# Two transformer layers on eight cores: background weight casts issued by a running account instead of by step counters, with the small loads around them moved

## Chip, cores, metric

One Trainium2 chip, all 8 cores, one launch. Each core takes one sample of the batch and runs the same program on it; nothing is exchanged. The metric is device time in microseconds (us) of the slowest core. Every core reads its weights from the chip's memory (HBM) itself, so the eight load at the same moments.

## The reference, cut to what matters

```python
for l in range(DEPTH):                                   # 2 layers; D=1024, 2048 latent + 256 context tokens
    sh1, sc1, g1, sh2, sc2, g2 = adaln(c, ada_w[l], ada_b[l])       # silu(c) @ w + b, six vectors; same for c_ctx
    mix_lat, mix_ctx = hybrid_mixer(modulate(x, ...), modulate(ctx, ...), ...)
    #  one input projection, 4 heads differential attention (2 softmax maps each, keys = latent + context)
    #  beside 4 heads bidirectional mLSTM (conv, gates, chunked scan); one output projection
    x = x + g1 * mix_lat
    x = x + g2 * channel_mixer(modulate(x, norm2_g[l], sh2, sc2), l, ...)
    #  layer 0: swiglu, D_FF=2816;  layer 1: top-2 of 8 experts, D_FF_EXPERT=3584
    ...                                                  # context tokens likewise, in layer 0 alone
```

The arithmetic is in bfloat16 on TensorE; all weights arrive as float32.

## The kernel before

**Stages.** Eight blocks of the modulation matrix and the input tokens are loaded, then each layer runs: `attn` (projection, norm and rotation of q and k in jobs of one head and one token tile, v in 18 blocks, then the attention proper), `w_out_half` (the attention half of the output projection), `mlstm` (eight projections `p` with a convolution each, gates, v and output gate blocks, then the scan of 18 chunks in two directions, which is 36 units `u` and 4 to drain), `w_out_norm` (the other half, together with the next norm). Layer 0 ends with `ffn_dense`, layer 1 with `moe_sparse`, in which tokens are routed by a float32 product with the router weights `wr`, scattered to slots in HBM (`xslots`), and 23 tiles of 256 slots go through the experts.

**The attention proper** walks over steps `g`: one step is one block of 128 keys against a tile of 512 queries of one head. TensorE makes two score blocks, ScalarE the exponential over both, TensorE eight products with `vaug`. A full tile is 18 steps; in layer 0 a context tile of 2 steps follows every four. Layer 0 has 296 steps, layer 1 has 288. At a tile's end VectorE divides by the sums (its `RECIPROCAL`, one in each tile). In layer 0 one of the 16 remaining blocks of the modulation matrix (`ada_half`, 16 small matmuls and a VectorE add) is worked in after every 17th step, from a single buffer `adaw` in the `attr` area: the load of the next one is issued right behind it.

**Background casts.** The experts' weights are needed in bfloat16, but come in float32. `precast` lets a DMA on the GpSimd (POOL) queue copy one block of 128x4096 from HBM to HBM and convert it: 2 MB read and 1 MB written. There are 168 of them (21 blocks of 8 experts), and the first load of an expert tile waits for the last. Each cast waits on POOL for the TensorE instruction recorded just before it, so it is issued where it stands in TensorE's order. Where they stand is set by counters in each loop: every fourth attention job, every 12th step in layer 0 and every 7th in layer 1, one after most projections `p`, every third scan unit up to `u` 27, one before each strip of the dense FFN, and so on. Whatever is left when `moe_sparse` begins is issued there in one go.

**Queues.** Weight loads (`wslot`, `fslot`, `adaw`, with a conversion to bfloat16) are issued on POOL too, in program order between the casts, and so are the `iota` table and `wr` at the start of `moe_sparse`, behind the casts that are left. SP has the input tokens, `lam`, the zero-fill of `xslots` (11.8 MB written from a small constant), and then the experts' weights. SP's instructions wait only for their own buffers: the zero-fill stands in `attn` of layer 1, but reads a constant that was loaded at the start.

A `fence` makes the named engines wait for all compute recorded so far. TensorE takes `wslot` slots in turn: in `mlstm` the projections with `p` from 4 on need the load of `w_in` group 4, which is issued at the start of `mlstm`, behind the casts of the attention.

## Time and profile before

| | us |
|---|---|
| median of 3 runs (lowest, highest) | 4913.67 (4563.16, 5036.57) |
| profiled execution | 4566.67 |
| its span on core 7, the slowest | 4565.6 |
| spans of the other cores | 4525.7 to 4563.2 |
| TensorE busy on core 7 | 3878.8 (85%) |
| VectorE, ScalarE, GpSimd busy | 1505.7, 1522.5, 523.0 |
| chain that ended last | PE 73%, ACT 7%, issue 6%, DVE 6%, DMA 4% |

The profile is one execution, and all rows below are of core 7 unless they say otherwise. "Issue" as a releaser is idle time of an engine for which the profile shows no wait. "Us to landing" of a DMA runs from its issue to its last byte. The experts' part begins near 2800 us and is the last 1,700 us of the span; all that is changed lies ahead of it.

### The profile page before, as it was taken

What the parts mean: (1) busy time and instruction counts of PE and PEld (TensorE: products, weight loads), DVE (VectorE), ACT (ScalarE), POOL (GpSimd) and SP (SyncE); (2) the same over time, 40 slices, a digit from 0 to 9 for tenths busy, and PEclk for the clock granted to TensorE, in tenths of its full rate; (3) what the DMA queues carried; (4) which work ended last, traced back from release to release, by engine and by line L of the source; (5) the groups of instructions that cost most, each with busy time, mean ns of one, the idle gap of its engine ahead of it and who ended that gap; (6) DMA issues with size and microseconds to landing.
All of it is one profiled execution on the core that took longest, in us unless ns stands there. A gap on an engine that the chain in (4) does not pass through costs nothing.

```text
span 4565.6 us, 77498 instructions; the slowest of 8 cores (4525.7 to 4565.6 us)
## 1 busy us (share of the span) xinstructions
PE 3878.8 (85%) x28584; PEld 2519.2 (55%) x28584; DVE 1505.7 (33%) x2750; ACT 1522.5 (33%) x2399; POOL 523.0 (11%) x634
## 2 busy tenths in 40 slices
PE   4788889657999979888695376999999999999994
PEld 2345545433444434554344255777777778787773
DVE  3634452673223264334127232111111111111114
ACT  4678822554010277884126231111111111111110
POOL 0210000540000012000007212000000000000003
PEclk8999999868999999998896567999999999999997
DMA  9586653648884526999947507999999999999997
GB/s 240 86 111 107 107 93 65 93 65 120 120 113 81 97 44 91 110 109 109 118 65 98 74 1 264 312 310 318 308 320 306 320 307 321 304 320 310 312 309 248
DMA packets 112689, 822.84 MB, mean 180 GB/s; under 512 B 14496, under 2 KB 14768, under 8 KB 41408
## 3 DMA queue, kind: packets, MB, share of 16 engines
q0 software_dynamic: 31392, 280.83, 40.2%
q1 hardware_dynamic: 80928, 537.05, 35.0%
q8 instruction: 237, 3.88, 0.4%
q14 instruction: 132, 1.08, 0.1%
HBM read 1016.79 MB, written 217.06 MB: 270 GB/s over the span
## 4 chain that ended last, share of the span: by engine, by line
PE 73%; ACT 7%; issue 6%; DVE 6%; DMA 4%; POOL 2%; another core or an unknown queue 2%; DVEq 0%; ACTq 0%; POOLq 0%; SPq 0%
PE psall L273 65%; PE psall L270 5%; ACT attr L298 4%; PE psall L277 2%; DMA adaw<-ada_w 2%; DMA xstage<-x 1%; DVE ntmp L301 1%; DVE attr L334 1%; ACT hT L298 1%; DVE attr L301 1%; POOL wslot L301 1%; DMA attr<-ada_w 1%; POOL sigt L301 1%; ACT wslot L298 1%
## 5 line engine op out<-in xcount | busy, mean ns | idle before, releaser
L273 PE MATMUL psall<-hs,mslot 128*128 128x256 bf16 x10304 | 1130.6, 273 | 0.5 <-ACT hs L332 0.5
L273 PEld LDWEIGHTS psall<-hs,mslot 128*128 128x128 bf16 x10304 | 1009.2, 98 | 123.0 <-issue 0.7
L298 ACT ACTIVATE sig<-psall 128x512 bf16<-128x512 f32 x322 | 192.2, 597 | 1444.7 <-PE psall L273 1444.7
L298 ACT ACTIVATE attr<-psall 128x1024 bf16<-128x1024 f32 (+1 forms) x660 | 592.1, 979 | 183.0 <-PE psall L273 180.4
L273 PE MATMUL psall<-mslot,ysp 128*128 128x512 bf16 x2576 | 559.7, 379 | 0.0
L301 DVE TENSOR_TENSOR ysp<-sig,psall 128x512 bf16<-128x512 bf16 x322 | 221.3, 687 | 866.4 <-PE psall L273 844.0
L270 PE MATMUL psall<-vaug,attr 128*128 128x129 bf16 x4640 | 393.1, 228 | 61.8 <-issue 29.3
L273 PEld LDWEIGHTS psall<-mslot,ysp 128*128 128x128 bf16 x2576 | 251.2, 98 | 298.5
L270 PEld LDWEIGHTS psall<-vaug,attr 128*128 128x128 bf16 x4640 | 278.0, 100 | 209.0 <-issue 207.4
L273 PE MATMUL psall<-hT,fslot 128*128 128x512 bf16 (+1 forms) x1760 | 352.0, 363 | 0.9 <-ACT ftf L298 0.9
L273 PE MATMUL psall<-hT,wslot 128*128 128x512 bf16 (+1 forms) x1248 | 282.6, 373 | 41.4 <-DMA wslot<-w_in 36.0
L273 PE MATMUL psall<-catA,kT 64*128 64x512 bf16 (+1 forms) x1440 | 272.6, 374 | 26.5 <-ACT attr L298 12.6
L273 PEld LDWEIGHTS psall<-hT,fslot 128*128 128x128 bf16 x1760 | 172.9, 99 | 176.6 <-issue 11.1
L328 DVE SCALAR_TENSOR_TENSOR xT<-psall,mod,xT 128x512 f32<-128x512 f32 (+1 forms) x264 | 185.7, 709 | 247.4 <-PE psall L273 237.9
L301 DVE TENSOR_TENSOR otok<-psall,g2b 128x512 bf16<-128x512 f32 x92 | 63.6, 692 | 534.2 <-PE psall L273 527.0
L1525 POOL DMA_DIRECT2D mwb<-mw x168 | 85.1, 507 | 1300.3 <-PE psall L273 1201.1
L273 PEld LDWEIGHTS psall<-hT,wslot 128*128 128x128 bf16 x1248 | 124.6, 100 | 173.6 <-issue 60.1
L298 ACT ACTIVATE ftf<-psall 128x512 f32<-128x512 f32 (+1 forms) x110 | 60.9, 554 | 444.3 <-PE psall L273 444.3
L371 POOL DMA_DIRECT2D oslots<-otok x23 | 16.8, 730 | 1672.9 <-PE psall L273 1454.8
L273 PE MATMUL psall<-wslot,hT 128*128 128x512 bf16 x848 | 191.2, 381 | 3.9 <-ACT vaug L332 3.9
L273 PE MATMUL psall<-y,fslot 128*128 128x512 bf16 (+1 forms) x880 | 179.0, 359 | 16.5 <-DVE xT L328 14.6
L301 DVE TENSOR_TENSOR y<-ftf,psall 128x512 bf16<-128x512 f32 (+1 forms) x110 | 69.6, 634 | 277.1 <-PE psall L273 274.3
(190 smaller groups left out, 3611.3 us busy)
## 6 DMA issues: line engine op xcount, KB each, us to landing
mslot<-mwb SPq DMA_DIRECT2D x483, 1024.0 KB, 6.8
mwb<-mw POOLq DMA_DIRECT2D x168, 1024.0 KB, 14.9
adaw<-ada_w POOLq DMA_DIRECT2D x32, 512.0 KB, 14.9
wslot<-w_in POOLq DMA_DIRECT2D x14, 1024.0 KB, 15.6
fslot<-f POOLq DMA_DIRECT2D x7, 2048.0 KB, 17.2
xslots<-cf SPq DMA_DIRECT2D x1, 11776.0 KB, 40.6
xst<-xslots POOLq DMA_DIRECT2D x23, 512.0 KB, 11.9
oslots<-otok POOLq DMA_DIRECT2D x23, 512.0 KB, 8.3
```

Source lines behind the costliest of these rows:

```text
L270: self.P.add("pe", lambda e: e.matmul(out.ap, lhsT.ap, rhs.ap, start=start, stop=stop, skip_group_check=True), reads=[lhsT, rhs], writes=[ ...
L273: self.P.add("pe", lambda e: e.matmul(out.ap, lhsT.ap, rhs.ap, start=start, stop=stop), reads=[lhsT, rhs], writes=[out])
L277: self.P.add("pe", lambda e: e.transpose(out.ap, in_.ap, ident.ap), reads=[in_, ident], writes=[out])
L298: self.P.add("act", lambda e: e.activation(out.ap, in_.ap, func, **kw), reads=rd, writes=wr)
L301: self.P.add(eng, lambda e: e.tensor_tensor(out.ap, in0.ap, in1.ap, op), reads=[in0, in1], writes=[out])
L328: self.P.add(eng, lambda e: e.scalar_tensor_tensor(out.ap, in0.ap, a, in1.ap, op0, op1), reads=rd, writes=[out])
L334: self.P.add(eng, lambda e: e.tensor_copy(out.ap, in_.ap), reads=[in_], writes=[out])
L371: return [e.dma_start(out=o, in_=i) for o, i in pairs]
L1525: idx = P.add("pool", lambda en, o=dst, i=src: [en.dma_start(out=o, in_=i)], dma=1, sembuf=self.mwb_buf)
```

## The change

Each stage now calls `pace(us)` at its TensorE work with a fixed number of microseconds for that piece: 2.7 for an attention job, 1.75 for a block of v, 1.05 for a step on a full tile, 2.5 and later 5.0 for a scan unit, 3.6 for an FFN strip. The sum is a credit; whenever it reaches `PACE` = 10.5, one cast is issued. Loads subtract from it: 3.0 for a modulation block, 6.0 for 128x4096 of `w_in` or `w_out`, 12.0 for an FFN block, 50.0 for the zero-fill. All counters of before are gone. The zero-fill of `xslots` moves into `mlstm` of layer 0, behind a fence on SP. `iota` and `wr` go to the SP queue in `mlstm` of layer 1, ahead of the scan, in a part of the slot area that the scan leaves free. A modulation block in the attention of layer 0 stands at the seventh step of each full tile.

```diff
+PACE = 10.5
...
+        self.pc_credit = 0.0
...
 def _ada_load(self, l, hb, wv):
     self.dma("pool", wv, DV(self.ada_w_d[l, hb, :, :], [Buf("d")]))
+    self.pc_credit -= 3.0
...                                          # attn
-    if l == 1:
-        zv = V(self.cf32.t[:, :].bitcast(BF16), self.cf32.v(0).bs)
-        nrow = MOE_TILES * MOE_T // 128
-        self.dma("sp", DV(self.xs_d[:, :].rearrange("(p r) d -> p r d", p=128), [self.xz_buf]),
-                 V(zv.ap.unsqueeze(1).to_broadcast([128, nrow, D]), zv.bs))
+    if l == 0:
+        self.pc_credit = 0.0
...                                          # v_blk, jobs
+        self.pace(1.75)
...
             stage_a(j)
+            self.pace(2.7)
...
-        if j % 4 == 1 and not nq - 6 < j < nq + 5:
-            self.precast(1)
...                                          # steps of the attention
         o_step(g)
+        self.pace(1.05 if steps[g][1] < 4 else 0.5)
...
-        if hbs and g % 17 == 16:
+        if hbs and steps[g][2] == 6 and steps[g][1] < 4:
...
-        if g % (12 if l == 0 else 7) == 6:
-            self.precast(1)
...                                          # _w_in_load, _w_out_load
+    self.pc_credit -= 6.0
...                                          # mlstm
     wk = self.w_in_load(l, w_in_d, 4)
+    if l == 0:
...
+        P.fence(("sp",))
+        self.dma("sp", DV(self.xs_d[:, :].rearrange("(p r) d -> p r d", p=128), [self.xz_buf]),
+                 V(zv.ap.unsqueeze(1).to_broadcast([128, nrow, D]), zv.bs))
+        self.pc_credit -= 50.0
...
                 proj(p, ti)
+                self.pace(2.7 if ti < 4 else 1.3)
...
-        if p < 8 and p != 4:
-            self.precast(1)
...
-    P.fence(("act", "dve", "pool"))
+    P.fence(("act", "dve", "pool", "sp") if last else ("act", "dve", "pool"))
+    if last:
+        self.wr = self.at("wr", [128, 8, 8], F32, OW + 15360)
+        self.iota_t = self.at("iota", [128, 32], F32, OW + 15616)
+        iota_d = self.din("iota", [128, 32])
+        self.dma("sp", self.iota_t.v(0), DV(iota_d[:, :], [Buf("d")]))
+        self.dma("sp", self.wr.v(0), DV(self.router_d[l // 2, :, :].rearrange("(k p) e -> p k e", p=128), [Buf("d")]))
...                                          # scan
     for u in range(NU + 4):
+        self.pace(2.5 if u < 18 else 5.0)
...
-        if u % 3 == 1 and u < 27:
-            self.precast(1)
...                                          # w_out_half, w_out_norm, ffn_dense: pace(1.1), pace(1.7), pace(3.6)
...
+def _pace(self, us):
+    self.pc_credit += us
+    while self.pc_credit >= PACE:
+        self.pc_credit -= PACE
+        self.precast(1)
...                                          # moe_sparse
-    self.dma("pool", iota_t.v(0), DV(iota_d[:, :], [Buf("d")]))
-    self.dma("pool", wr.v(0), DV(router_d[l // 2, :, :].rearrange("(k p) e -> p k e", p=128), [Buf("d")]))
```

**The order on POOL, attention of layer 1.** `mwb<-mw` is a cast, `sigt` and the second `wslot<-w_in` are the loads at the start of `mlstm`. Before:

```order
L1525 DMA mwb<-mw 32x16384
L371 DMA wslot_45<-w_out 128x4096
L371 DMA wslot_45<-w_in 128x4096
L1525 DMA mwb<-mw 32x16384 x44
L371 DMA sigt_73<-w_in 128x128
L371 DMA wslot_45<-w_in 128x4096
L1525 DMA mwb<-mw 32x16384 x4
```

Now:

```order
L302 TENSOR_TENSOR attr_70<-attr_70 128x512 x2
L372 DMA wslot_45<-w_out 128x4096
L372 DMA wslot_45<-w_in 128x4096
L1534 DMA mwb<-mw 32x16384 x31
L372 DMA sigt_73<-w_in 128x128
L372 DMA wslot_45<-w_in 128x4096
L1534 DMA mwb<-mw 32x16384 x4
```

Between the two loads at the attention's start and those at the start of `mlstm` stand 31 casts where 44 stood.

**The order on POOL, end of the scan of layer 1** (`sigt<-tmpo` are the last scan units, `h2f<-nhf` is routing). Before:

```order
L301 TENSOR_TENSOR sigt_73<-tmpo_74,sigt_73 128x512 x5
L1525 DMA mwb<-mw 32x16384 x8
L371 DMA iota_88<-iota 128x32
L371 DMA wr_87<-router_w 128x8x8
L334 CAST h2f_86<-nhf_89 128x512 x32
```

Now:

```order
L1534 DMA mwb<-mw 32x16384
L302 TENSOR_TENSOR wslot_45<-vaug_47,ga_75 128x516
L302 TENSOR_TENSOR sigt_73<-tmpo_74,sigt_73 128x512
L302 TENSOR_TENSOR wslot_45<-wslot_45,gd_77 128x516
L302 TENSOR_TENSOR wslot_45<-vaug_47,ga_75 128x516
L302 TENSOR_TENSOR sigt_73<-tmpo_74,sigt_73 128x512 x5
L335 CAST h2f_88<-nhf_89 128x512 x32
```

The last cast is issued inside the scan, nothing is left for the start of `moe_sparse`, and `iota` and `wr` are on SP ahead of the scan.

**The order on POOL, start of the attention of layer 0** (`attr<-ada_w` is a modulation block). Before:

```order
L1525 DMA mwb<-mw 32x16384
L371 DMA wslot_45<-w_out 128x4096
L371 DMA wslot_45<-w_in 128x4096
L371 DMA attr_55<-ada_w 128x2048
L1525 DMA mwb<-mw 32x16384
L371 DMA attr_55<-ada_w 128x2048
```

Now:

```order
L302 TENSOR_TENSOR attr_55<-attr_55 128x512 x2
L372 DMA wslot_45<-w_out 128x4096
L372 DMA wslot_45<-w_in 128x4096
L372 DMA attr_55<-ada_w 128x2048 x2
L1534 DMA mwb<-mw 32x16384
L372 DMA attr_55<-ada_w 128x2048
```

The first modulation block is still loaded third in the row, but it is used at step 6 where it was used at step 16; the next two are loaded before the first cast of the attention.

## Rows read from the trace of the kernel before

**Rows 1.** Span and mean granted clock of core 5

```profile
core 5: 4558.4 us, clock 0.910
```

**Rows 2.** TensorE's waits, whole span: in total us, times, longest us

```profile
PE psall L270 <- DMA wr<-router_w: 46.9, 1, 46.9
```

**Rows 3.** TensorE's waits, 2118 to 2300 us (start of `mlstm`, layer 1)

```profile
PE psall L273 <- DMA wslot<-w_in: 36.0, 1, 36.0
...
PE psall L273 <- issue: 6.0, 1, 6.0
```

**Rows 4.** POOL's `wslot` loads, 2150 to 2215 us: count, first and last issue, landing

```profile
L371 POOL DMA_DIRECT2D wslot<-w_in x2: 535/550/564, 2155.1 to 2207.0; - x2
...
DMA to landing us min/median/max: 75.4/80.5/85.6
```

**Rows 5.** Casts (L1525), 1785 to 2158 us, the attention of layer 1

```profile
L1525 POOL DMA_DIRECT2D mwb<-mw x44: 491/491/506, 1790.3 to 2151.5; - x44
...
DMA to landing us min/median/max: 26.1/61.8/89.7
```

**Rows 6.** Casts, 300 to 600 us, the attention of layer 0

```profile
DMA to landing us min/median/max: 8.0/11.0/13.3
```

**Rows 7.** Stretches inside both attentions: busy us by engine, then PEclk, DMA share, GB/s

```profile
350.00:600.00 250.00, 217.15 (x2436) 136.40 (x2436) 104.90 (x213) 210.29 (x251) 15.53 (x30) 0.95 0.63 105
...
1850.00:2100.00 250.00, 209.99 (x2133) 126.81 (x2130) 84.59 (x154) 201.87 (x232) 14.26 (x29) 0.92 1.00 109
```

**Rows 8.** TensorE's waits, 1783 to 2118 us, the attention of layer 1

```profile
PE psall L270 <- issue: 26.4, 12, 4.1
PE psall L273 <- issue: 6.6, 2, 3.7
```

**Rows 9.** TensorE's waits, 262 to 601 us, the attention of layer 0

```profile
PE psall L270 <- issue: 2.8, 2, 1.6
```

**Rows 10.** VectorE's timeline: tile ends in layer 1's attention, the first two and the last (16th)

```profile
1801.23 0.20 DVE L354 RECIPROCAL rzs<-attr 128x8 f32<-128x8 f32 x1
...
1819.19 0.20 DVE L354 RECIPROCAL rzs<-attr 128x8 f32<-128x8 f32 x1
...
2117.64 0.20 DVE L354 RECIPROCAL rzs<-attr 128x8 f32<-128x8 f32 x1
```

**Rows 11.** Casts, 2538 to 2546 us, start of `moe_sparse`

```profile
L1525 POOL DMA_DIRECT2D mwb<-mw x8: 491/498/557, 2540.8 to 2544.2; - x8
...
DMA to landing us min/median/max: 13.0/42.1/57.4
```

**Rows 12.** Timeline, POOL and TensorE: first modulation block in the attention of layer 0

```profile
262.05 0.55 POOL L371 DMA_DIRECT2D attr<-ada_w  x1
...
289.17 0.56 PE L273 MATMUL psall<-scb,attr 128*128 128x2 bf16 x16 [12.09 <-DMA attr<-ada_w]
```

**Rows 13.** TensorE's waits, 1055 to 1090 us, start of the dense FFN

```profile
PE psall L273 <- DMA adaw<-ada_w: 5.7, 2, 3.4
```

**Rows 14.** The zero-fill on SP: issue, landing

```profile
L371 SPq DMA_DIRECT2D xslots<-cf x1: 617/617/617, 78.4 to 78.4; - x1
...
DMA to landing us min/median/max: 40.6/40.6/40.6
```

**Rows 15.** POOL's `wslot` loads, 636 to 692 us (`mlstm`, layer 0), and TensorE at `p` 4

```profile
L371 POOL DMA_DIRECT2D wslot<-w_in x2: 532/542/552, 640.2 to 690.7; - x2
...
DMA to landing us min/median/max: 12.3/13.4/14.5
...
689.48 1.89 PE L273 MATMUL psall<-hT,wslot 128*128 128x512 bf16 x8
```

**Rows 16.** TensorE's waits on core 5, whole span

```profile
PE psall L273 <- DMA wslot<-w_in: 39.6, 1, 39.6
PE psall L270 <- DMA wr<-router_w: 34.9, 1, 34.9
PE psall L270 <- issue: 30.8, 15, 3.8
```

More of the change, by code:

```diff
@@ L391, in build @@
         f2_d = [self.din(f"f2_{g}", [128, min(8, D_FF // 128 - g * 8) * D]) for g in range(3)]
-        router_d = self.din("router_w", [1, D, NEXP])
+        router_d = self.router_d = self.din("router_w", [1, D, NEXP])
         self.mw_d = [self.din(f"mw_{b}", [NEXP, 128, 4096]) for b in range(21)]
@@ L1027, in _w_out_load @@
     self.dma("pool", V(wv, wb), DV(w_out_d[l, half, :, :], [Buf("d")]))
+    self.pc_credit -= 6.0
     return wv.rearrange("p (k c) -> p k c", c=1024), wb
@@ L1055, in _mlstm @@
     wk = self.w_in_load(l, w_in_d, 4)
+    if l == 0:
+        zv = V(self.cf32.t[:, :].bitcast(BF16), self.cf32.v(0).bs)
+        nrow = MOE_TILES * MOE_T // 128
+        P.fence(("sp",))
+        self.dma("sp", DV(self.xs_d[:, :].rearrange("(p r) d -> p r d", p=128), [self.xz_buf]),
+                 V(zv.ap.unsqueeze(1).to_broadcast([128, nrow, D]), zv.bs))
+        self.pc_credit -= 50.0
     for i in range(2):
@@ L1145, in _mlstm @@
         bank = ps[5 + blk % 3]
+        self.pace(1.75)
         wv, wb = wv_
@@ L1151, in _mlstm @@
         self.copy(V(vaug.t[:, blk, :, 0:128], vaug.v(("v", blk)).bs), srcv, eng="act" if blk % 2 == 0 else "dve")
-        if blk == 8:
-            self.precast(1)
     P.fence(("dve",))
@@ L1164, in _mlstm @@
         bank = ps[blk % 4]
+        self.pace(1.75)
         wv, wb = wo_
@@ L1171, in _mlstm @@
         self.tt(sig.v(blk, ALL, blk, ALL), tv, mgb, ALU.mult)
-        if blk % 6 == 3:
-            self.precast(1)
-    P.fence(("act", "dve", "pool"))
+    P.fence(("act", "dve", "pool", "sp") if last else ("act", "dve", "pool"))
[5 more added lines that the diff above has]
+        self.dma("sp", self.wr.v(0), DV(self.router_d[l // 2, :, :].rearrange("(k p) e -> p k e", p=128), [Buf("d")]))
     hsum = Tn(hT.t[:, :, :].rearrange("p a b -> p (a b)").bitcast(F32).rearrange("p (a b) -> p a b", b=512), "hsum")
@@ L1326, in _mlstm @@
                     V(g.ap.unsqueeze(2).to_broadcast([128, 4, 129]), g.bs), ALU.mult, eng="pool")
-        if u % 3 == 1 and u < 27:
-            self.precast(1)
         if live and i == 14 and d == 1:
@@ L1348, in _w_out_half @@
             cnt += 1
+            self.pace(1.1 if ti < 4 else 0.5)
             for k in range(4):
@@ L1353, in _w_out_half @@
             self.stt(xv, bank.v(0, ALL, S(0, n)), modv(2, m, s), xv, ALU.mult, ALU.add)
-        if m in (1, 3, 6):
-            self.precast(1)
 def _w_out_norm(self, w, out_tiles, modv, gen_fn):
@@ L1370, in _w_out_norm @@
             cnt += 1
+            self.pace(1.1 if ti < 4 else 0.5)
             for k in range(4):
@@ L1382, in _w_out_norm @@
                 pass
-        self.precast(1)
         gen = gen_fn(ti)
@@ L1424, in load @@
         self.dma("pool", sv, DV(src[:, :], [Buf("d")]))
+        self.pc_credit -= 12.0
         views.append(sv)
@@ L1431, in w2_unit @@
         cntB += 1
+        self.pace(1.7 if ti < 4 else 0.9)
         bO = ps[4 + cntB % 2]
@@ L1451, in _ffn_dense @@
                     cntA += 1
+                    self.pace(3.6 if ti < 4 else 1.8)
                     par = cntA % 2
@@ L1467, in _ffn_dense @@
                         w2_unit(sv, wv, ng, m, ti)
-                    if m % 4 == 1:
-                        self.precast(1)
                 continue
@@ L1511, in _ffn_side @@
         self.ada_load(1, hb, aw.v(hb % 2, ALL_, hb % 2, ALL_))
-    self.precast(1)
 Builder.ffn_side = _ffn_side
@@ L1530 @@
 Builder.precast = _precast
+def _pace(self, us):
[3 more added lines that the diff above has]
+        self.precast(1)
+Builder.pace = _pace
 def _moe_sparse(self, l, w, out_tiles, router_d, ABv, modv):
@@ L1537, in _moe_sparse @@
     self.precast(len(self.pc_list))
-    iota_d = self.din("iota", [128, 32])
     keep = OC + 16384
@@ L1547, in _moe_sparse @@
     h2f = self.at("h2f", [128, 8, 512], BF16, OW)
-    wr = self.at("wr", [128, 8, 8], F32, OW + 8192)
-    iota_t = self.at("iota", [128, 32], F32, OW + 8448)
+    wr, iota_t = self.wr, self.iota_t
     nhf = self.at("nhf", [128, 2, 512], F32, OR + 11264)
-    self.dma("pool", iota_t.v(0), DV(iota_d[:, :], [Buf("d")]))
-    self.dma("pool", wr.v(0), DV(router_d[l // 2, :, :].rearrange("(k p) e -> p k e", p=128), [Buf("d")]))
     pR = ps[7]
```

## The prediction

> **What bounds the kernel now.** I read the cores first. All eight end within 40 us of each other, core 7 last at 4565.6 and core 5 close behind [rows 1]. The chain that ended last is TensorE for 73% of the span. The experts' part, from 2800 us on, is not touched. Ahead of it I looked at what TensorE waits for, and where. Three waits are for a DMA that was issued in time but landed late: 46.9 us for the router weights [rows 2], 12.1 us for a modulation block [rows 12], 36.0 us for the `w_in` load of `mlstm` in layer 1 [rows 3]. The reader is to see that none of these transfers is large: the `w_in` loads took 75 to 86 us to land [rows 4], where a load of the same size in layer 0 took 12 to 15 [rows 15]. What they wait behind is casts. In the attention of layer 1, 44 casts go out from 1790.3 us on and the time to landing climbs from 26.1 to 89.7 us [rows 5]. In the attention of layer 0 it stays between 8.0 and 13.3 us [rows 6]. The stretches say the same: DMA share 1.00 in the one, 0.63 in the other [rows 7].
>
> The queue's own price per cast follows from rows 5. The first landed at 1790.3+26.1 = 1816.4, the last at 2151.5+80.0 = 2231.5 (I take 80.0 for the last from the load right behind it, whose median is 80.5 [rows 4]). Over 43 intervals that is 9.65 us for each cast on a full queue. Before, one was issued in (2151.5-1790.3)/43 = 8.4 us: 1.25 us too fast, 44 times, and 26 us to begin with make some 80 us of backlog.
>
> A fourth loss is spread. The same attention has 33.0 us of "issue" gaps on TensorE [rows 8], in which the profile shows no wait. Its first tile took 1819.19-1801.23 = 17.96 us; all 15 from there to the last took 316.4, or 21.09 each [rows 10]. 15 x 3.13 = 47 us are lost against a clean tile, the 33.0 of gaps and what follows each of them: the granted clock in this stretch is 0.92, a mix of its two levels 2.4 and 1.2 GHz, against 0.95 in layer 0 [rows 7]. Layer 0 has nearly the same GB/s (105 against 109) and 2.8 us of such gaps [rows 9], so I tie the gaps to the full queue, which is an inference from two stretches and not shown.
>
> **The change, part by part.** The sum is made against the profiled execution, 4566.67 us, 1.1 above its span. It stands beside the lowest of the three runs (4563.16); the median is 347 us higher, and the forecast is for executions like the profiled one.
>
> *Router weights.* They leave a place behind 8 casts, the last of which lands 57.4 us after its issue [rows 11], for one some 180 us earlier. Their wait, 46.9, goes. Next is the ScalarE result that the same product reads. During the stall two of those were made ahead, so I count 45 (bounds 40 and 47). The Trainium skill ("DMA: Bandwidth & Descriptors", on issuing engines not being separate DMA queues) speaks against a gain from the other queue as such: transfers of SP and POOL run on the same 16 DMA engines and interleave. By that rule it is the earlier place that pays, and by the rule or without it the term is the same as long as the place is before the scan.
>
> *The w_in load of layer 1.* 31 casts stand where 44 stood. Some three of them belong to `w_out_half`; in the attention one is issued every 10 steps (10.5/1.05), which on clean tiles (17.96/18 = 1.00 us a step) is 10.0 us. A full queue needs 9.65, so no backlog grows. The load then lands in about 13 us as in layer 0 [rows 15]. It was issued at 2155.1 and landed 85.6 us later [rows 4], and TensorE had waited for 36.0 of them [rows 3]: it is needed 49.6 us after its issue. Gone: 36.0, and the one gap of 6.0 behind it [rows 3]. Bounds 36 and 42, since nothing else is close.
>
> *The attention of layer 1.* Between nothing, if the gaps come from load as such (10.0 us between casts is 97% of the queue's rate), and 47, if they come from backlog. Nearest is layer 0, with 2.8 us of gaps at nearly the same GB/s [rows 7, 9]; but its queue empties now and then, at a DMA share of 0.63. I take 34.
>
> *The attention of layer 0.* The first modulation block is used at step 6 instead of 16. Its load is third in a row of three behind the last cast; it was issued at 262.05 and TensorE went on at 289.17 [rows 12]. Those loads stand in the same order, so they land when they did. TensorE had made 17 steps in 15 us by then and will have made 7: 10 steps of 0.9 us are done after the stall and not before it. Cost 8 to 9 us; less if the casts before it end earlier (bounds 0 and 12). I take 8. The other 15 blocks have a tile's time, 18 us, against 8 to 13 us to land: nothing.
>
> *Dense FFN.* The load of the second block with two modulation blocks behind it stood behind a fifth cast in `w_out_norm`; now there are four, and it can go out about 15 us sooner. That removes the 5.7 [rows 13]. The two later waits of this kind follow the FFN loads themselves, which stay where they are: nothing. I take 6.
>
> *Zero-fill.* Issued at 78.4 us it ran for 40.6 us [rows 14], between the input tokens and the first cast, so its old place cost nothing. Its new place has the `w_in` load of `mlstm` beside it. That load landed at 640.2+12.3 = 652.5; behind the whole zero-fill it would be 693, and TensorE needs it at 689.5 [rows 15]. Cost 0 to 4 us of waiting, and up to 6 us of gaps like those of rows 8; I take 0, since the two queues share and no cast is issued for about 50 us.
>
> *Casts in other places.* In the scan's second half about eight stand where one stood. POOL spends 0.5 us on each [rows 5], at most 4 us in a layer if none of it is hidden; it is busy for 11% of the span, so I take 0. The projections ahead of the first attention get 12 casts for 9; each waits for TensorE's job and then holds POOL 0.5 us, ahead of a multiply. Bounds 0 and 1.5, and I take 0.
>
> *Sum, core 7:* -45 -36 -6 -34 +8 -6 = -119, so 4566.7-119 = 4448. *Core 5* has less to lose: 39.6, 34.9 less 2, gaps of which I again take 32, and 5 behind the load [rows 16], with the same +8 and -6: 4558.4-33-39.6-32-5+8-6 = 4451, and 1 for what lies around the span. The slowest core decides: **4450 us**, 2.6% less than 4566.67. A measurement of this kernel can tell about 2%, which is 91 us: 4475.
>
> **Rivals.**
>
> 1. *The gaps stay.* If 97% load is as bad as a full queue, the attention of layer 1 gives nothing: 4450+34 = 4484, and the stalls alone are won. For it: the casts are 10.0 us apart against 9.65 of service, no more than 4% of slack, and every waiting TensorE delays the next cast but not the queue. Against: layer 0's landings of 8 to 13 us [rows 6]. By the Trainium skill ("HBM Reference", the table at its head) a core has about 358 GB/s; by that a cast's 3.15 MB would take 8.8 us and the slack would be 12%, and the attention would give nearly all of the 47, for 4437. The trace has 9.65, and that is what the sum goes by.
>
> 2. *Slower.* The account spreads the load so evenly that the queue is nearly full everywhere, and the "issue" gaps with it. Price: 33.0 us of gaps in 335 us [rows 8] over the 2400 us in which casts run would be 236 us in place of 39, so +197. With the two stalls won (81, and 6 in the FFN) and 8 lost it ends at 4566.7+197-87+8 = 4685. It decides from where more than 40% of that stretch has such gaps. Against: the same 168 casts take 168 x 9.65 = 1621 us of 2400, and only the attentions and the FFN loads lie near the queue's rate.
>
> 3. *The change doesn't do what it says.* The credit counts work at fixed prices. Where TensorE is faster than its account, casts bunch up as before: in the v blocks ahead of each attention 6 casts go out in about 50 us, 8.5 us apart. Against 9.65 of service that is 7 us of backlog; the first block of layer 0 lands 7 us later, and two tiles of each attention may show gaps of 2 us more: 4450+7+8 = 4465.
>
> 4. *More is won.* No gaps in layer 1 (13 more) and none at the first block (8 more): 4429.
>
> **How the numbers follow.** The forecast, with its own spread of 4437 to 4463, 0.52. Rival 1, 4468 to 4492, 0.20. Rival 3, 0.10. Rival 4, 0.13. Rival 2, 0.05. Forecast, rival 3 and rival 4 make 0.75, so the range needs most of rival 1 too: 4424 to 4488. Under 4475 lie those 0.75 and a small part of rival 1: 0.77 faster by over 2%. The rest of rival 1 is within 2%: 0.19. Slower: 0.04, rival 2 without its mildest part.
>
> **What the changed profile would show.** Right: no wait of TensorE for `wr` and none for `wslot<-w_in` over 5 us; casts in the attention of layer 1 landing within 20 us, with DMA share under 0.95; its 15 tiles near 18.8 us; a wait for `attr<-ada_w` of some 20 us at step 6. Wrong: landings that still climb in either attention; a wait for `wslot` near 690 us, beside the zero-fill; "issue" gaps in stages that had none. The forecast fails if those gaps have another cause than the queue, or if a wait behind the removed ones, such as routing, grows by what was won.

## The result, and the profile after

The changed kernel took 4441.76 us in the median of four executions (4438.91 to 4918.51). Against the kernel before, run on the same chip, the ratio is 0.973 (95% interval 0.9701 to 0.9758): faster by 2.7%, where the forecast was 2.6% and 4450 us. The near agreement of the two is in part luck, as the table below shows. The median of before in the table above holds executions with a disturbed die; comparisons here leave such executions out.

The profiled execution took 4442.59 us, 124.1 less than the 4566.67 that the sum was made against. All cores, in answer to [rows 1]:

```profile
core 3: 4441.5 us, clock 0.922
...
core 7: 4431.3 us, clock 0.923
die 0 (median of its cores): 4433.4 us, clock 0.922
die 1 (median of its cores): 4435.0 us, clock 0.923
```

Core 3 is last now, 5 to 11 us behind the others; before, it was the second fastest of the eight. Rows of after are of core 3 from here on. TensorE's waits over the whole span, first those for a DMA or "issue" (in us: total, times, longest), in answer to [rows 2, 3, 8, 9, 12, 13]:

```profile
PE psall L278 <- issue: 27.4, 4, 9.9
...
PE psall L274 <- DMA attr<-ada_w: 14.2, 1, 14.2
...
PE psall L274 <- DMA adaw<-ada_w: 13.1, 4, 6.3
...
PE psall L274 <- DMA wslot<-w_in: 4.7, 2, 3.2
...
PE psall L274 <- issue: 0.4, 2, 0.2
...
PE psall L271 <- issue: 0.3, 1, 0.3
```

The wait for `wr` is gone. What is left for `wslot<-w_in` is not at `mlstm` but at the v weights of both layers (3.2 at 199 us, 1.5 near 1720 us). The "issue" gaps of the attention (L270 before, L271 now) fell from 26.4 in layer 1 (33.0 with the 6.6 at L273) and 2.8 in layer 0 to 0.3. All cores show it: in the attention of layer 1 they had 31 to 43 us of such gaps before and have at most 0.8 now. `attr<-ada_w` is 14.2 on core 3 and 14.9 on core 7, which had 12.1 before.

The casts (L1534) between 1790 and 2080 us, in answer to [rows 5]:

```profile
L1534 POOL DMA_DIRECT2D mwb<-mw x28: 491/491/506, 1799.0 to 2071.8; - x28
...
DMA to landing us min/median/max: 7.6/8.0/13.7
```

They are (2071.8-1799.0)/27 = 10.1 us apart and land after a median of 8.0 us where it was 61.8. From the third on, a cast has landed before the next one is issued. The `wslot` load at the start of `mlstm`, in answer to [rows 4], landed in 13.6 us where it took 85.6:

```profile
L372 POOL DMA_DIRECT2D wslot<-w_in x1: 532/532/532, 2112.7 to 2112.7; - x1
...
DMA to landing us min/median/max: 13.6/13.6/13.6
```

The same stretches inside both attentions, in answer to [rows 7] (the second is 50 us shorter, since the attention ends earlier). The granted clock of the second rose from 0.92 to 1.00, the 2.4 GHz level throughout, and the DMA share fell from 1.00 to 0.57 at nearly the same GB/s:

```profile
350.00:600.00 250.00, 220.23 (x2512) 138.62 (x2510) 106.13 (x216) 216.63 (x259) 16.11 (x31) 0.97 0.64 108
1850.00:2050.00 200.00, 187.00 (x2046) 116.07 (x2043) 81.12 (x145) 189.83 (x225) 9.83 (x20) 1.00 0.57 107
```

Tile ends in the attention of layer 1, the first two and the last, in answer to [rows 10]: 272.4 us for 15 tiles, 18.16 each, where it was 21.09.

```profile
1802.86 0.20 DVE L355 RECIPROCAL rzs<-attr 128x8 f32<-128x8 f32 x1
1820.82 0.20 DVE L355 RECIPROCAL rzs<-attr 128x8 f32<-128x8 f32 x1
...
2075.30 0.20 DVE L355 RECIPROCAL rzs<-attr 128x8 f32<-128x8 f32 x1
```

The zero-fill, in answer to [rows 14], and the loads beside it, in answer to [rows 15]: the fill has taken 44.3 us for 40.6, and the `wslot` loads landed in 8.1 and 11.3 us, sooner than before.

```profile
L372 SPq DMA_DIRECT2D xslots<-cf x1: 617/617/617, 644.5 to 644.5; - x1
...
DMA to landing us min/median/max: 44.3/44.3/44.3
...
L372 POOL DMA_DIRECT2D wslot<-w_in x2: 527/530/533, 644.1 to 693.9; - x2
...
DMA to landing us min/median/max: 8.1/9.7/11.3
```

**Where the time went.** Every TensorE instruction of the trace of before was matched with the same one of the same core after, to see how the lag between them moves. The first columns are core 7; the last one has the lowest and the highest step of all eight cores. This table is worked out from the traces and is no view of the profile:

```
stretch of before, us            lag after it   step    forecast    step, eight cores
   0 -  262  up to attention 0        +0.9       +0.9      0          +0.5 to  +6.9
 262 -  300  its first block          +3.8       +2.9     +8          +2.9 to  +9.8
 300 -  606  rest of attention 0      -2.2       -6.0      0          -9.3 to  -2.2
 606 - 1055  mlstm 0, zero-fill       +2.3       +4.5      0          -4.5 to  +4.5
1055 - 1310  dense FFN               -10.1      -12.4     -6         -13.9 to  +2.9
1310 - 1600  rest of the FFN         -10.7       -0.6      0          -0.9 to  +0.4
1600 - 1783  ahead of attention 1     -1.7       +9.0      0          +2.5 to  +9.0
1783 - 2125  attention 1             -48.1      -46.4    -34         -55.8 to -39.4
2125 - 2270  w_in of mlstm 1         -93.0      -44.9    -42         -44.9 to -23.8
2270 - 2541  rest of mlstm 1         -95.4       -2.4      0          -3.5 to  +1.3
2541 - 2602  router weights         -140.3      -44.9    -45         -45.0 to -30.9
2602 - 2750  routing                -141.6       -1.3      0          -1.5 to  +1.3
2750 - 2800  start of the experts   -136.9       +4.7      0          -4.0 to  +4.7
2800 - end                          -134.3       +2.6      0          -1.4 to  +6.1
```

The spans fell by 130, 106, 122, 89, 89, 125, 116 and 134 us on cores 0 to 7. The cores that had waited longest for the queue gained most, and their spread shrank from 40 us to 11.

### The profile page after: what moved, and what is told of

It is laid out like the page before. It is cut to its first block, busy times and chain, and to the rows that moved or that the text cites. A ratio compares the mean times of both kernels' runs of the same rounds, so it can differ in the third digit from the quotient of the medians.

```text
span 4441.5 us, 77519 instructions; the slowest of 8 cores (4430.9 to 4441.5 us)
## 1 busy us (share of the span) xinstructions
PE 3862.1 (87%) x28584; PEld 2511.8 (57%) x28584; DVE 1504.3 (34%) x2750; ACT 1518.7 (34%) x2399; POOL 521.6 (12%) x632
## 4 chain that ended last, share of the span: by engine, by line
PE 72%; ACT 9%; issue 6%; DVE 6%; DMA 4%; POOL 2%; ACTq 0%; DVEq 0%; another core or an unknown queue 0%; POOLq 0%; SPq 0%
PE psall L274 66%; ACT attr L299 6%; PE psall L271 4%; PE psall L278 2%; DMA xstage<-x 1%; DVE attr L335 1%; DVE ntmp L302 1%; DMA adaw<-ada_w 1%; ACT hT L299 1%; DMA wslot<-w_in 1%; POOL wslot L302 1%; ACT wslot L299 1%; DVE attr L302 1%; POOL sigt L302 1%; POOL gath L1810 0%
## 5 line engine op out<-in xcount | busy, mean ns | idle before, releaser
L271 PE MATMUL psall<-vaug,attr 128*128 128x129 bf16 x4640 | 381.0, 224 | 37.1 <-DVE attr L335 34.3
L271 PEld LDWEIGHTS psall<-vaug,attr 128*128 128x128 bf16 x4640 | 270.4, 99 | 181.1 <-issue 179.8
L1534 POOL DMA_DIRECT2D mwb<-mw x168 | 85.8, 510 | 1384.2 <-PE psall L274 1290.8
## 6 DMA issues: line engine op xcount, KB each, us to landing
xslots<-cf SPq DMA_DIRECT2D x1, 11776.0 KB, 44.3
```

Source lines behind the costliest of these rows:

```text
L271: self.P.add("pe", lambda e: e.matmul(out.ap, lhsT.ap, rhs.ap, start=start, stop=stop, skip_group_check=True), reads=[lhsT, rhs], writes=[ ...
L1534: idx = P.add("pool", lambda en, o=dst, i=src: [en.dma_start(out=o, in_=i)], dma=1, sembuf=self.mwb_buf)
```

## Experiments

Ten kernels on three chips, with one of them on two of these. Ratios are to the kernel before on the same chip, where it took 4571 to 4597, 4582 to 4593 and 4561 to 4570 us. To tell runs of different chips apart, ratios are compared and not times.

**Does the rate of casts in layer 1's attention make the gaps?** The changed kernel with the old counter there:

```diff
-        self.pace(1.05 if steps[g][1] < 4 else 0.5)
+        if l == 0:
+            self.pace(1.05 if steps[g][1] < 4 else 0.5)
+        elif g % 7 == 6:
+            self.precast(1)
```

> The changed kernel with one part undone: in the attention of layer 1 a cast at every 7th step again, in place of the account. Everything else stays, so the router weights are still early. Theory (a queue fed faster than it empties, so that every later transfer on it, the 16 KB instruction packets among them, waits behind casts): landings climb to 70 us or more, TensorE has about 33 us of issue gaps there and 15 tiles take near 316 us, and the w_in load of mLSTM costs 30 to 40 us again. In all 75 to 95 us over the changed kernel: 4517 to 4537. Rival (the gaps came from something else that the change moved, such as where casts stand in POOL's order): the tiles stay near 18 us, and at most the w_in wait of some 36 us comes back, 4478.

Measured: median 4530.67 us, ratio 0.9881 (0.9835 to 0.9926), some 69 us over the changed kernel by the ratios (0.015 x 4584), a little less than the 75 to 95 expected. TensorE's waits on core 7, the casts in this attention, and its stretch:

```profile
PE psall L271 <- issue: 34.8, 17, 5.0
...
PE psall L274 <- issue: 15.0, 6, 6.3
PE psall L274 <- DMA wslot<-w_in: 12.3, 3, 5.1
```

```profile
L1537 POOL DMA_DIRECT2D mwb<-mw x44: 491/491/542, 1785.9 to 2179.6; - x44
...
DMA to landing us min/median/max: 16.7/49.0/71.6
```

```profile
1850.00:2100.00 250.00, 208.44 (x2058) 126.17 (x2059) 80.17 (x144) 194.14 (x223) 14.25 (x29) 0.90 1.00 109
```

Gaps, share and clock are back, with everything else in the changed kernel's form. The gaps are even worse than in [rows 7, 8]: the 15 tiles took 334.2 us (their ends lie at 1815.39 and 2149.63), where 316 had been expected. The `w_in` load is late too, 54.4 us to landing, but at the start of `mlstm` TensorE waited for only 4.8 of them, not the 30 to 40 expected. The casts are issued by TensorE's steps, and the slower TensorE spread them: (2179.6-1785.9)/43 = 9.2 us apart, not 8.4, so the backlog ended smaller. What the backlog costs moved from the wait behind it to the gaps inside it.

**Are two edits the whole gain?** The kernel before with a cast at every 10th step in layer 1, the casts so saved in `mlstm`, and the router weights on SP:

```diff
-        if g % (12 if l == 0 else 7) == 6:
+        if g % (12 if l == 0 else 10) == 6:
...
-        if blk == 8:
+        if blk in (2, 8, 14):
...
-        if blk % 6 == 3:
+        if blk % 3 == 0:
```

> The kernel before with two edits and no account: in the attention of layer 1 a cast every 10th step in place of every 7th, the casts so saved partly put into mLSTM (v blocks and output gate), and the router weights and iota on SP before the scan. Theory: the whole gain comes from these two. Tiles of 18 us, no wait for w_in, none for the router weights: 45 + 44 + 44 = 133 us under before, 4432 to 4445, equal to the changed kernel within 10 us, since its account then adds only the few us of the dense FFN. Rival (the account matters as such, through an even load in all stages): 30 us or more over the changed kernel.

Measured: 4461.51 us, ratio 0.9739 (0.9704 to 0.9774), the changed kernel's within the interval. Its casts in this attention, 332.0/32 = 10.4 us apart:

```profile
L1531 POOL DMA_DIRECT2D mwb<-mw x33: 491/491/542, 1787.6 to 2119.6; - x33
...
DMA to landing us min/median/max: 7.9/11.9/25.3
```

A counter at a wider step does what the account does there. "Issue" in the attentions is 8.9 us in all, 3.7 of them in layer 1. The interval leaves room for a difference of some 16 us either way.

**The router weights alone**, on the kernel before (`iota` and `wr` by SP ahead of the scan, as in the change):

```diff
-    self.dma("pool", wr.v(0), DV(router_d[l // 2, :, :]...
...                                          # mlstm, ahead of the scan
+        self.dma("sp", self.wr.v(0), DV(self.router_d[l // 2, :, :]...
```

> The kernel before with the router weights and iota on SP before the scan, nothing else. The 8 casts that are left still go out at the start of the experts' part. Theory: the wait of 33 to 47 us for the router weights goes and nothing takes its place, since the 8 casts land some 100 us before the experts' first tile: 35 to 45 us under before, 4520 to 4530. Rival (what was hidden behind it appears, or the cores that waited less decide): less than 25 us.

Measured: 4545.95 us, ratio 0.9912 (0.9876 to 0.9948), 40 us, with all else as before. Core 4's waits:

```profile
PE psall L270 <- issue: 34.6, 18, 3.3
PE psall L273 <- DMA wslot<-w_in: 33.2, 1, 33.2
```

So what is left to the other edit is (0.9912-0.9739) x 4584 = 79 us, with some 20 either way, for one number in one loop and the saved casts put elsewhere: the stall at `w_in` and the gaps together.

**The zero-fill at its old place**, in the changed kernel:

```diff
...                                          # attn, layer 0
+        self.dma("sp", DV(self.xs_d[:, :].rearrange("(p r) d -> p r d", p=128), [self.xz_buf]),
+                 V(zv.ap.unsqueeze(1).to_broadcast([128, nrow, D]), zv.bs))
...                                          # mlstm, layer 0
-        P.fence(("sp",))
-        self.dma("sp", DV(self.xs_d[:, :]...
```

> The changed kernel with the zero-fill of the slots issued at its old place, in effect at about 78 us; the account still subtracts its 50 so that every cast stays where it is. Theory: the zero-fill is hidden at both places; within 5 us of the changed kernel. Rival (its new place costs, through the w_in load beside it or through gaps in TensorE's instructions): 5 to 15 us faster than the changed kernel. Other rival (its old place cost something in the first norm): slower by that.

Measured: 4461.49 us, ratio 0.9726 (0.968 to 0.9771). No difference, though the interval of some 21 us either way could not have told the 5 to 15 us of the rival. The traces can: from 640 to 760 us, where the zero-fill now runs, cores 0, 3 and 7 of the two kernels differ by 0.2 us or less by the same matching, and core 5 by 1.5. From 60 to 200 us, its old place, they differ by 0.6, -0.3, 2.9 and 1.3. It is hidden in both places, within some 3 us.

**The changed kernel unaltered**, on the second chip, as the measure for the next three:

> The changed kernel itself, unaltered, as the measure for the three beside it on the same chip: 0.973 of before, 110 to 135 us less.

Measured: ratio 0.9711 (0.9687 to 0.9734), from two executions, 4454.31 and 4452.65 us.

**The modulation blocks of layer 0 at every 17th step again:**

```diff
-        if hbs and steps[g][2] == 6 and steps[g][1] < 4:
+        if hbs and g % 17 == 16:
```

> The changed kernel with the modulation blocks of the attention of layer 0 after every 17th step again. Theory of the prediction: the first block then waits 10 steps later for a load that lands at the same moment, so 7 to 9 us are won back at the attention's start: 4 to 9 us faster than the changed kernel. Rival, from the trace of the changed kernel (the stretch from the entry to the end of that attention got 3 to 5 us shorter in spite of the earlier first block): blocks inside the tiles save in the tiles after a context tile, which took 21 to 22 us and now take 20 to 21, about what the entry costs; then the two are within 3 us.

Measured: 4455.42 us, ratio 0.9705 (0.9678 to 0.9732): no difference in all. On core 5 the wait for the first block is half as long (16.8 in the changed kernel), but 5.4 us of gaps stand beside it:

```profile
PE psall L274 <- DMA attr<-ada_w: 8.3, 1, 8.3
...
PE psall L271 <- issue: 5.4, 3, 3.3
```

Matched with core 5 of the changed kernel, the first block is 9.4 us cheaper, about the theory's 7 to 9, and the rest of that attention 9.6 dearer, which is the rival's point.

**Small loads first.** TensorE's remaining DMA waits in layer 0 are all for modulation blocks behind larger loads. In the changed kernel, the first block goes ahead of the `w_out` and `w_in` loads of the attention, and an FFN load goes behind the two modulation blocks of its first strip:

```diff
+    if hbs:
+        self.ada_load(0, hbs[0], adaw.v(0))
     wo = self.w_out_load(l, w_out_d, 0)
     wq = self.w_in_load(l, w_in_d, 3)
-    if hbs:
-        self.ada_load(0, hbs[0], adaw.v(0))
...                                          # ffn_dense
-        if q + 1 < len(loads):
+        if q + 1 < len(loads) and kind == 1:
             load(q + 1)
...
                 self.ffn_side()
+                if jj == 0 and q + 1 < len(loads):
+                    load(q + 1)
```

> The changed kernel with two orders of loads turned round: the first modulation block of the attention of layer 0 ahead of the two 128x4096 loads, and in the dense FFN the two modulation blocks ahead of the FFN load at the start of each weight block. Theory: these waits are transfers queued behind bigger ones that nobody needs yet. The 14 us wait at the attention's start falls under 5, the 13 us of waits for adaw in the FFN go: 18 to 25 us faster than the changed kernel. Rival: the FFN load, which gets out 1 to 20 us later behind a block that must wait for TensorE, is then late itself and takes part of it back.

Measured: 4424.18 us (4416.7 to 4425.9), ratio 0.9641 (0.962 to 0.9662), against 0.9711 for the changed kernel on the same chip: 0.007 x 4586 = 32 us, where 18 to 25 had been expected, and the best version of all. Waits of core 1:

```profile
PE psall L274 <- DMA wslot<-w_in: 8.1, 2, 4.1
PE psall L274 <- DMA attr<-ada_w: 4.0, 1, 4.0
PE psall L274 <- issue: 0.6, 2, 0.5
PE psall L274 <- DMA adaw<-ada_w: 0.2, 1, 0.2
```

Both waits are all but gone. By the same matching against the changed kernel (cores 1, 2 and 7) 12 to 13 us come at the first block of the attention and 14 to 18 in the FFN. The first of these is the wait that the forecast had put at some 20 us; it was a matter of the order of three loads.

Once more, on a third chip:

> The kernel with the first modulation block loaded ahead of the two weight loads of the attention, and the modulation blocks ahead of the FFN loads, once more on the chip of the two other runs of this call. Theory: the 32 us under the changed kernel on an earlier chip are from the order of loads and not from that chip: a ratio to the kernel before of 0.960 to 0.968 again. The rival: they were in good part the chip's, and the ratio is 0.968 to 0.973.

Measured: 4412.56 us, ratio 0.9664 (0.9641 to 0.9688). It holds.

**The 9 us ahead of layer 1's attention.** The version above, with the account read at the end of a job behind POOL's multiply, and no cast in the eight jobs around the v weights' load:

```diff
-            self.pace(2.7)
...
+        if j < len(jobs) and nq - 4 < j < nq + 5:
+            self.pc_credit += 2.7
+        elif j < len(jobs):
+            self.pace(2.7)
```

> As e8_small_first, and in the projections ahead of each attention the account is read at the end of a job, behind the multiply on POOL, and no cast goes out in the eight jobs around the load of the v weights. Theory: this stage of layer 1 is 7 to 9 us longer in the changed kernel than before, 0.5 us for each cast that holds POOL ahead of the multiply (five of them) and 3 to 5 us of waiting for the v weights, which stand behind a cast: another 6 to 9 us faster in layer 1 and 2 to 5 in layer 0, so 25 to 35 us faster than the changed kernel. Rival: two casts in one go behind the eight jobs meet the loads of the attention and give some of it back; then it is equal to e8_small_first.

Measured: 4437.18 us, ratio 0.9671 (0.9647 to 0.9695), about 14 us slower than the version it starts from, though the two intervals touch; 25 to 35 us under the changed kernel had been expected. The 9 us shrank as meant (6.7 less there on core 7, and no wait for `wslot`), but the credit saved up in layer 0 was paid out at once. Casts from 195 to 262 us, first of this kernel, then of the version without it:

```profile
L1541 POOL DMA_DIRECT2D mwb<-mw x8: 501/546/550, 201.3 to 252.3; - x8
...
DMA to landing us min/median/max: 13.4/26.3/30.5
```

```profile
L1536 POOL DMA_DIRECT2D mwb<-mw x7: 542/547/549, 199.1 to 255.9; - x7
...
DMA to landing us min/median/max: 9.1/13.2/17.8
```

One cast more in a shorter time doubled the landings, and the first modulation block, behind them, was waited for again:

```profile
285.79 0.56 PE L274 MATMUL psall<-scb,attr 128*128 128x2 bf16 x16 [17.94 <-DMA attr<-ada_w]
```

Against the changed kernel the first block gains nothing now (0 to 4 us lost on cores 0, 2, 6 and 7). The attention of layer 1 loses too, 9 to 16 us on the same cores: its gaps are back, 8.3 us on core 0 and 7.8 on core 7, behind casts that took up to 21 and 25 us to land. This is rival 3 of the prediction, bunching in the v blocks, brought about by a saved-up credit; in the changed kernel itself it isn't there.

**The later reading alone**, in the changed kernel, for the jobs and the v blocks beside them, no cast held back:

```diff
             stage_a(j)
-            self.pace(2.7)
...
             stage_c(j - 2)
+        if j < len(jobs):
+            self.pace(2.7)
```

> The changed kernel with the account read at the end of each attention job, behind the job's multiply on POOL, instead of ahead of it; the same pieces and prices, no cast held back. Theory: in the projections ahead of the attention of layer 1 the steps of 0.5 us, one for each cast that holds POOL ahead of a multiply, go (some 3 us in all), and the 4.8 us at the v weights stay, since their load still stands behind a cast. The same in layer 0, 2 to 4 us. In all 3 to 7 us faster than the changed kernel, too little for the interval and to be read in the trace. The rival: the late reading bunches the casts ahead of layer 0's attention, as it did when it was tried together with the casts held back, and gives back as much or more at the first modulation block: no gain or up to 8 us slower.

Measured: 4453.92 us, ratio 0.9764 (0.974 to 0.9787). No gain. In the traces of cores 3, 5 and 7 1.8 to 2.4 us are won from 1655 to 1710 us, and 1.5 to 5.0 are lost again up to 1725 us; TensorE still waits 3.8 us for `wslot<-w_in` there on core 5.

**How near the queue's limit may the casts come?** The changed kernel with

```diff
-PACE = 10.5
+PACE = 9.0
```

> The changed kernel with PACE 9.0 in place of 10.5: a cast for each 9.0 us of the account, which on clean tiles of layer 1's attention (1.05 for a step of 1.00 us) is one in 8.6 us, where the full queue needed 9.65 for each and where the kernel before issued one in 8.4. My theory: the full-queue price holds, so backlog grows by some 1.1 us a cast over about 36 casts, to 40 us and more; landings climb from below 15 to above 45 us, instruction gaps (issue) of TensorE come back in this attention, 20 to 35 us of them, and its 15 tiles take 295 to 320 us against 272. The w_in load of mlstm lands late by the same backlog; TensorE needs it some 50 us after issue, so 0 to 10 us of wait. Layer 0's attention, with a modulation block in each tile beside two casts, is near the queue's rate too and may show up to 10 us of gaps. In all 25 to 55 us slower than the changed kernel. The rival: a cast that finds the queue empty was seen to land in 7.7 us, and if that is what the queue can do at any load, 8.6 us between casts leaves 10% of slack: landings stay under 15 us, no gaps, the time within 8 us of the changed kernel's. The second rival of the prediction (a queue near full everywhere puts gaps everywhere) would have over 100 us more here.

Measured: 4528.62 and 4528.76 us, two executions and no interval; against the mean of before on the same chip, 4565.25, that is 0.992. Its casts and TensorE's waits from 1775 to 2140 and 1765 to 2110 us, and two stretches, core 4:

```profile
L1534 POOL DMA_DIRECT2D mwb<-mw x37: 491/491/547, 1780.7 to 2135.9; - x37
...
DMA to landing us min/median/max: 9.4/21.3/30.6
```

```profile
PE psall L271 <- issue: 22.4, 10, 4.5
PE psall L274 <- issue: 5.8, 3, 2.1
```

```profile
350.00:600.00 250.00, 213.22 (x2368) 133.46 (x2367) 99.97 (x201) 205.70 (x244) 17.16 (x33) 0.93 0.91 117
1900.00:2100.00 200.00, 167.78 (x1683) 101.95 (x1682) 65.60 (x119) 159.04 (x183) 9.33 (x19) 0.91 0.99 111
```

28.2 us of gaps and 313.4 us for the 15 tiles (first and last end at 1849.69 and 2163.05) lie in what was expected; the rival, with no gaps, is refuted. Three things were not as expected. The backlog did not reach 45 us. Most of it came ahead of the attention, beside the v blocks, where seven casts went out 7.0 us apart and the landings rose from 13 to 28 us. From 1848 to 1892 us, with casts 8.7 us apart, they went from 26 to 31. Then the slowed TensorE issued casts 10.2 us apart, and the landings fell to 14 by 2070 us, while gaps of up to 4.5 us went on. Second, layer 0's attention, for which I had allowed 10 us, cost 22 to 35 by the matched instructions of cores 1, 3 and 4, at a DMA share of 0.91 where the changed kernel has 0.64. Third, the whole was 82 to 91 us over the changed kernel by the spans of these cores (87 by the ratios), and not 55. By its tiles layer 1's attention lost 41.0 of the 44.0 us that the change had won there.

**What the gaps are.** The profile names nothing for them, so I laid the packets of the `instruction` DMA queue (q8 on the page, 16384 bytes each) beside them. Read from the trace, core 7 of before, us:

```
packet starts    1858.2  1872.4  1886.5  1901.9  1915.9  1929.5  1944.5  1958.5  1969.9  1984.7
  and takes         1.5     1.3     1.0     1.8     1.6     1.6     1.3     1.4     1.3     1.4
issue gap from   1856.9  1874.4  1886.6  1901.3    -     1930.6  1945.3  1959.8    -     1984.2
        to       1861.0  1874.7  1888.8  1904.9    -     1932.6  1947.2  1961.1    -     1987.5
```

Each of the eight gaps lies over or right behind such a packet. The same holds for all 14 gaps of this attention, for the 20 with the old counter in the changed kernel, and with PACE 9.0 for all 13 from 1879 to 2094 us: each gap ends 2.2 to 3.1 us after a packet starts, whatever its length. The changed kernel has 23 such packets on core 3 between 1819 and 2073 us and not one gap of over 0.3 us. The program's instructions come by the same 16 DMA engines as the casts (the page counts 237 packets of this queue in after); the reading is that where casts are queued, TensorE runs out of instructions before the next packet is there. That the packets are late because of casts is inferred from these positions and from the three runs in which the backlog was changed (the old counter, the step of 10, PACE 9.0); no row shows when a packet was asked for.

## Where the prediction failed, and what of it was right

**The step that failed** is the term for the attention of layer 1, -34. Its bounds were right: 47 if backlog is the cause, which it is, and nothing if the load as such were. The 34 between them was a discount for "10.0 us between casts is 97% of the queue's rate", and no run supports a discount. It was -46.4 on core 7, and -39.4 to -55.8 over the eight cores. A cast that finds the queue empty lands in 7.6 to 8.0 us, so at 10.0 us between casts the queue empties before each one; the stretch shows a DMA share of 0.57. A second step failed beside it. The projections ahead of layer 1's attention had no term at all; only those ahead of the first attention were weighed, with bounds of 0 and 1.5. They cost +9.0 on core 7 and 2.5 or more on every core.

**And the total was near by luck.** On core 7 the terms missed by some -37 us in one direction and +22 in the other, which left -134 for -119. The step "the slowest core decides" was worked out for cores 7 and 5 alone: 4448 and 4451 were forecast, and they ended at 4431.3 and 4433.8. The 4441.5 that decided is core 3's, a core that had waited less before and gained only 89 us. So the last line of the sum is 8 us off because a core that was not looked at gained less than the two that were.

*Router weights, -45.* Right on core 7: -44.9. The other cores gained 31 to 42, and alone on the kernel before it is 40 us in the slowest core. `wr` landed in 2.3 us on SP. By the Trainium skill ("DMA: Bandwidth & Descriptors", on issuing engines not being separate DMA queues) the other queue is no gain as such; no run here put `wr` on SP at its old place, so that part stays untested.

*The `w_in` load, -36 and -6.* Right on core 7: -44.9, of which 38.0 at the stall and 6.4 at the gap behind it. The cores that had waited 14 to 19 us for this load gained 24 to 27. The experiment with the old counter shows that the sum holds only for both losses of the backlog together: the same 44 casts after a less loaded start cost 4.8 us there, and more in gaps.

*Attention of layer 1, -34 between 0 and -47.* The mechanism was right, and the two experiments on the step show it; the size was off, as said above. The price of the full queue, 9.65 us, is still what decides where backlog begins: with PACE 9.0 the landings rose from 26 to 31 us at 8.7 us between casts, where a queue that needs 7.6 would have drained, and they fell at 10.2 us. By the Trainium skill ("HBM Reference", the table at its head) a core has about 358 GB/s, by which a cast's 3.15 MB would take 8.8 us, an estimate. The runs have 7.6 alone and 9.65 in a row, so neither agrees.

*First modulation block of layer 0, +8.* Right in kind, and too much for core 7: +2.9, where the eight cores have 2.9 to 9.8. The reason was named ("less if the casts before it end earlier"). On core 3 the load was issued at 267.47 and landed 19.7 us later, where it had been 27.0 on core 7 of before, because the last cast ahead of it was issued 12.1 us earlier (255.39) and had been 4.7 (257.38 for 262.05). Moving the blocks back gained 9.4 us at this block, as forecast, and lost it again in the tiles; moving the load to the front of its row brought 12.

*Rest of that attention, 0.* -6.0. I had left out the 2.8 us of gaps in [rows 9] as noise of a healthy stage; they went too. The place of the modulation blocks has a share in it: on core 5, which had gained 9.3 here, the experiment with the old place lost 9.6, of which 5.4 are gaps.

*Dense FFN, -6.* Undersized on core 7: -12.4. The first wait, 5.7 us long, was worth 8.3. The second cost 1.1 more, and the third got 5.2 shorter: its blocks landed in 16.2 and 18.7 us where they took 20.1 and 23.9, behind an FFN load that took 13.8 us and not 17.2. That the FFN loads "stay where they are" was true of their order and not of what was still queued when they were issued. Cores 0, 2, 5 and 7 gained 12 to 14 us here; they had waited 23 us for these blocks. The other four had waited 13 to 15, and they stayed within 3 us of before.

*Zero-fill 0, other casts 0.* The zero-fill is right, by the run with it at its old place. The scan's casts are too: of the +4.5 in `mlstm` of layer 0 at most 0.6 are in the scan, and layer 1 has -2.4. The projections ahead of the first attention got 0 to 1.5, and the stretch up to it cost 0.9 on core 7, though up to 6.9 on others. Those ahead of layer 1's attention got nothing and cost +9.0. In the trace it is 1.8 at 1608 us, four steps of some 0.6 where a cast holds POOL ahead of a multiply, and 4.9 where the v weights' load now stands behind a cast. I had counted the hold on POOL and forgotten the load behind it on the queue, which was my own rule for moved steps. Neither attempt to win it back made the kernel faster.

*Start of the experts, 0.* +4.7 on core 7 and between -4.0 and +2.8 on the others. The cores have two shapes there, before and after alike: cores 4 to 7 wait 28 to 32 us for `xst<-xslots`, and cores 0 to 3 have 29 to 35 us in pieces, "issue" among them (the 27.4 of the view above is core 3). The change made neither. What the pieces are stays open; no cast runs there.

*Rivals.* The first (gaps stay) and the second (gaps everywhere, slower) are refuted for PACE 10.5; with 9.0 the gaps of the first do come, and spread to layer 0. The third showed only where it was forced, by a saved-up credit and by PACE 9.0. The fourth, more is won, was the nearest to what happened in both its places on core 7, though not in its time, since another core decided.

## What to carry to other kernels

Background transfers should be spaced by what the queue needs when full, with a few per cent to spare: at 10.0 us for 9.65 they left TensorE without gaps, and at a nominal 8.6 (7.0 us apart in one stage, 8.7 and then 10.2 in the next) they cost 80 to 90 us of 4450. The profile shows it as a DMA share near 1.00 and as "issue" gaps of an engine that waits for nothing. One step number and one early small load did the whole of this change within what can be measured; the account behind it is only a way to keep the spacing. Then look at who stands in a row with whom: the smallest load that is needed first goes first, and that gave another 32 us. And when the slowest core decides, work the sum out for all of them: terms read on the slowest one were up to twice what others had to win.

## What the runs showed of the hardware

Instruction packets of 16 KB travel over the same DMA engines as data, one each 10 to 15 us in the attention. Behind a queue of one to three casts (landings of 14 to 31 us with PACE 9.0) TensorE has gaps of up to 4.5 us, and each of the 47 gaps counted ends 2.2 to 3.1 us after such a packet starts. The granted clock of such a stretch is 0.90 to 0.92 and not 1.00. Such a backlog limits itself in part when the casts are tied to TensorE's steps, because the slowed TensorE issues them further apart. At 9.2 us between casts the landings still climbed, to 72 us in 44 casts; at 9.9 on average they rose to 31 and fell again. A converting copy of 128x4096 takes 7.6 us alone and 9.65 in a row, though the first figure includes its start and end. I had expected the lone one to take longer. Whether the row is slower because the other cores' copies run at the same moments, no run here separates.
